# Where the rows of an expert norm are permuted: by the multiply that writes them, or by the transposes that read them

## The chip, the cores and the metric

The kernel runs on one core of one Trainium2 chip. The metric is the device time of one execution in microseconds (us). The core's engines are named as in the profile: PE is TensorE (PEld are its weight loads, which overlap with its matmuls), DVE is VectorE, ACT is ScalarE, POOL is GpSimd, SP issues most of the DMA transfers.

## The reference

A decoder trunk of two layers on x of 512 tokens by 1024 features, all float32. Each layer is a mixer (layer 0: mLSTM heads beside differential attention; layer 1: a gated convolution), then a mixture of experts, each behind an RMSNorm; a last RMSNorm ends it. What matters here is the part around the experts, cut:

```python
h = rmsnorm(x, norm_ffn[layer])            # y = x * rsqrt(mean(x*x) + eps) * g
glog = t @ wg + bg                         # t = h as 512 x 1024; 4 groups
elog = t @ we + be                         # 16 experts, 4 per group
# top-1 group, then top-2 experts within it, softmax weights
for e in range(16):
    y = (silu(t @ w_gate[e]) * (t @ w_up[e])) @ w_down[e]   # 1024 -> 512 -> 1024
    out = out + combine[:, e:e + 1] * y
x = x + out
```

## The kernel before

Tokens lie in four tiles of 128 rows (`TT = 4`), the features in eight blocks of 128 (`KD = 8`). PE contracts over partitions, so each normed tile, token by feature, has to be turned: eight 128 by 128 transposes, each of which loads one block of the tile as weights (a PEld instruction) and streams an identity through it.

There are five norms, n = 0 to 4. The even ones stand ahead of the mixers and at the end. The odd ones, n = 1 and n = 3, are the expert norms. The weights of gate, up and router are fetched with `rearrange("(p k) n -> p k n")`: partition p holds the features 8p to 8p + 7, so block k of the contraction is every eighth feature, k, k + 8, k + 16, and so on. The odd norms therefore write their rows permuted: the DVE multiply of `norm` (one scalar_tensor_tensor per tile, line 913) reads x and the gain in order and writes feature 8p + k at position 128k + p of `h_rows`, neighbouring results 512 bytes apart. Everything after it reads blocks of 128 contiguous columns:

* `turn_h(n, t)` (line 1386) turns tile t, for the routing logits (`logits`, line 1607). For the odd norms it is called in `project_out`, between the tiles of the mixer's output projection: tiles (1,0), (1,1), `turn_h` 0, tile (1,2), `turn_h` 1, `logits` 0, tile (1,3), `turn_h` 2, `logits` 1, `turn_h` 3, `logits` 2 and 3.
* POOL stores the four tiles to `h_dram` (line 514). After routing it gathers, for each expert, up to 96 of those rows (`CAP = 96`) by an indirect DMA into `xg` (line 521), two buffers in turn.
* `turn_xg(n, u)` (line 1650) turns the 96 gathered rows of one expert, eight transposes of 96 by 128. ACT copies the result out of PSUM rounded to fp32r (line 743), DVE subtracts to get the remainder (line 1237).

A projection is three fp32r matmuls (`mm3`, lines 1404 to 1406): high by high, low by high, high by low. The weights come in as float32 by SP into a ring, ACT rounds each chunk (line 569) and DVE takes the remainder (line 875).

One step of the expert loop on PE, written out by hand in `step`: the gate matmuls of expert e, `turn_act` of e - 1, the up matmuls of e, `turn_xg` of e + 1, the down matmuls of e - 1. There are 16 experts per layer and two layers, so 32 calls of `turn_xg`, 256 transposes; `turn_h` of the odd norms has 8 calls, 64 transposes.

A branch for experts with more than 96 tokens (line 1731) has the same transposes.

Of the kernel before, what the change touches and what calls it, by code (L numbers as in the profile page):

```python
# [31 lines left out]
P = 128  # L32
# [3 lines left out]
KD = D // P  # L36
# [8 lines left out]
CAP = 96  # L45
# [27 lines left out]
def hybrid_trunk(nc, A, out):  # L73
    ctx = ExitStack()
    with ctx:
# [12 lines left out]
        ident = sb("ident", [P, P])  # L88
# [60 lines left out]
        h_rows = part(0, TT, D)  # L149
# [14 lines left out]
        xg = part(8192, 2, D)  # L164
# [224 lines left out]
        def turn_bank(n, t):  # L389
            return 2 * (t % (2 if n else 3))  # L390
# [465 lines left out]
        def _(dve):  # L856
# [27 lines left out]
            def norm(n, finish_x=None, ahead=0, copies=True):  # L884


                def copy(t):
                    b, cs = turn_bank(n, t), slice(t * P, (t + 1) * P)
                    if n % 2 == 0:
                        dve.wait_ge(tr_act, n * TT + t + 1)  # L890
                        ins = v.tensor_tensor(hT[:, 1, :, cs], ps[:, b:b + 2, :].rearrange("p b (k c) -> p (b k) c", k=4),
                                              hT[:, 0, :, cs].bitcast(F32), ALU.subtract)
                    else:
                        dve.wait_ge(tr_full, 2 * (n * TT + t) + 2)
                        ins = v.tensor_copy(hT_route[:, 4:8, cs], ps[:, b + 1, :].rearrange("p (k c) -> p k c", k=4))
                    ins.then_inc(tr_dve, 1)

                if finish_x and ahead:
                    finish_x(0)
                for t in range(TT):  # L900
                    if finish_x and t + ahead < TT:
                        finish_x(t + ahead)
                    if t == 0 and n == 0:
                        dve.wait_ge(first_gain_loaded, 16)
                    elif t == 0:
                        dve.wait_ge(gain_loaded, 16 * n)
                    dve.wait_ge(norm_rstd, n * TT + t + 1)
                    row, h_row, gains = x_sb[:, t, :], h_rows[:, t, :], gain[:, :]
                    if n % 2:

                        row, gains = (a.rearrange("q (p k) -> q p k", k=KD) for a in (row, gains))
                        h_row = h_row.rearrange("q (k p) -> q p k", k=KD)
                    ins = v.scalar_tensor_tensor(out=h_row, in0=row, scalar=st[:, 4 + t:5 + t],  # L913
                                                 in1=gains, op0=ALU.mult, op1=ALU.mult)
                    ins.then_inc(h_ready, 1)
                    if copies and t and n:
                        copy(t - 1)
                if n == 0:

                    copy(0)  # L920
                    splits(2)
                    copy(1)
                    splits(PIECE)
                    copy(2)
                    splits(at_start(0))
                    copy(3)
                elif copies:
                    copy(TT - 1)
# [444 lines left out]
        def _(pe):  # L1373
            mm = nc.tensor.matmul

            def turn_h(n, t):

                pe.wait_ge(h_ready, n * TT + t + 1)
                reuse = 2 if n else 3
                if t >= reuse:  # L1380
                    pe.wait_ge(tr_act, n * TT + t + 1 - reuse)
                    pe.wait_ge(tr_dve, n * TT + t + 1 - reuse)
                for b in range(2):
                    for k in range(4):
                        c = 4 * b + k
                        last = nc.tensor.transpose(ps[:, turn_bank(n, t) + b, k * P:(k + 1) * P],  # L1386
                                                   h_rows[:, t, c * P:(c + 1) * P], ident[:, :])
                    last.then_inc(tr_full, 1)

            def norm(n):  # L1390
# [235 lines left out]
            def route(l):  # L1626
# [10 lines left out]
                for e in range(E):  # L1637
# [5 lines left out]
                    if e % 4 == 3:  # L1643
                        last.then_inc(idx_full, 1)

            def turn_xg(n, u, landed_value):

                pe.wait_ge(xg_landed[u], landed_value)
                for k in range(KD):
                    last = nc.tensor.transpose(ps[:, 5 + k // 4, (k % 4) * P:(k % 4) * P + CAP],  # L1650
                                               xg[0:CAP, u, k * P:(k + 1) * P], ident[0:CAP, 0:CAP])
                last.then_inc(xg_turned, 1)

            def gate_or_up(bank, u, c, i):
# [33 lines left out]
            def experts(l):  # L1688
                n0, c0 = E * l, step_chunk(l, 0)
                turn_xg(n0, 0, 16 * (n0 // 2 + 1))  # L1690
                gate(n0, 0, c0, None)
                turn_xg(n0 + 1, 1, 16 * (n0 // 2 + 1))
                gate_or_up(1, 0, c0 + 4, None)

                def step(n, u, c, i, landed_next, first=False, last=False):

                    gate(n, u, c, i)
                    turn_act(n - 1)
                    gate_or_up(1, u, c + 4, i)
                    if not last:  # L1700
                        turn_xg(n + 1, 1 - u, landed_next)
                    down(n - 1, 1 - u, c + 8, i, first)

                for e in (1, 2):
                    n = n0 + e
                    step(n, e % 2, step_chunk(l, e), None, 16 * ((n + 1) // 2 + 1), first=(l == 0 and e == 1))
                with pe.Fori(0, E // 2 - 2) as i:
                    for u in range(2):
                        step(i * 2 + (3 + u + n0), 1 - u, step_chunk(l, 3) + 12 * u, i,
                             i * 16 + 16 * ((4 + u + n0) // 2 + 1))  # L1710
                n = n0 + E - 1
                step(n, 1, step_chunk(l, E - 1), None, None, last=True)
                turn_act(n)
                down(n, 1, step_chunk(l, E), None)

                o = over[l]
                pe.wait_ge(flag_ready, l + 1)
                with pe.If(pe.value_load(overflow_flag[0:1, l:l + 1], min_val=0, max_val=1) > 0):
                    pe.wait_ge(y_act, n0 + E)
                    pe.wait_ge(y_dve, n0 + E)  # L1720
                    with pe.Fori(0, E * OVER) as it:
                        w8 = w_over.rearrange("p (k n) -> p k n", k=KD)
                        w4 = w_over.rearrange("p (k n) -> p k n", k=KF)
                        pe.wait_ge(o["sel"], it + 1)
                        for t in range(TT):
                            last = mm(ps[0:CAP, 0, 0:1], sel_over[:, t, 0:CAP], tok_id[:, t:t + 1],
                                      start=(t == 0), stop=(t == TT - 1))
                        last.then_inc(o["idx_full"], 1)
                        pe.wait_ge(o["xg"], it * 16 + 16)
                        for k in range(KD):  # L1730
                            last = nc.tensor.transpose(ps[:, 1 + k // 4, (k % 4) * P:(k % 4) * P + CAP],
                                                       xg[0:CAP, 0, k * P:(k + 1) * P], ident[0:CAP, 0:CAP])
                        last.then_inc(o["turned"], 1)
                        pe.wait_ge(o["xgT"], it + 1)
                        for m in range(2):
                            pe.wait_ge(o["w"], it * 48 + 16 * (m + 1))
                            for k in range(KD):
                                last = mm(ps[0:CAP, 3 + m, :], xgT_over[:, k, 0:CAP], w8[:, k, :],
                                          start=(k == 0), stop=(k == KD - 1))
                            last.then_inc(o["done"], 1)  # L1740
                        pe.wait_ge(o["act"], it + 1)
                        for k in range(KF):
                            last = nc.tensor.transpose(ps[:, 5, k * P:k * P + CAP], act_h[0:CAP, k * P:(k + 1) * P],
                                                       ident[0:CAP, 0:CAP])
                        last.then_inc(o["act_turned"], 1)
                        pe.wait_ge(o["actT"], it + 1)
                        pe.wait_ge(o["w"], it * 48 + 48)
                        for half in range(2):
                            for k in range(KF):
                                last = mm(ps[0:CAP, 6 + half, :], actT_over[:, k, 0:CAP], w4[:, k, half * 512:half * 512 + 512],  # L1750
                                          start=(k == 0), stop=(k == KF - 1))
                        last.then_inc(o["done"], 1)
# [39 lines left out]
```

## Time and profile before

| | |
|---|---|
| median of 3 runs | 1253.16 us (1252.01 to 1254.99) |
| the profiled execution | 1254.11 us, its span 1252.4 us |
| PE busy | 1088.5 us, 87% of the span |
| DVE busy | 864.5 us, 69% |
| ACT busy | 655.3 us, 52% |
| granted PE clock, mean over the span | 0.917 |
| HBM | 267.57 MB read, 20.20 MB written |

The span is the part of the execution that the profiler records, 1.7 us less than the execution's time. Busy shares are means over stages that differ: the two expert loops, from about 375 to 660 us and from about 923 to 1210 us, are nearly half of the span. The granted clock is given as a share of 2.4 GHz: 1.00 is 2.4 GHz and 0.50 is 1.2 GHz. Durations of PE instructions contain a latency that overlaps with the next instruction, so the pace, start to start, says what a row of them costs.

### The profile page before, as it was taken

To read this page: it belongs to the slowest core of one execution; us is meant where nothing else is said; L and a number is where in the kernel's file an instruction comes from. 1 tells how busy PE (TensorE), PEld (TensorE's weight loads), DVE (VectorE), ACT (ScalarE), POOL (GpSimd) and SP (SyncE) were. 2 spreads that over 40 slices of the span, in tenths; PEclk is the share of its full clock that TensorE was granted. 3 is DMA by queue.
4 is the path that set the end of the run, shared out by engine and by line. 5 is a ranking of instruction groups with operands and counts; after the bars stand their busy time and mean duration, and the time that the engine had idled before them with its cause. 6 is when DMAs were issued, how large, how long until landed. Compare 5 with 4: busy or idle time off the path is not lost.

```text
span 1252.4 us, 14773 instructions
## 1 busy us (share of the span) xinstructions
PE 1088.5 (87%) x5104; PEld 819.8 (65%) x5104; DVE 864.5 (69%) x1067; ACT 655.3 (52%) x809; POOL 115.3 (9%) x159
## 2 busy tenths in 40 slices
PE   5999994896958999999993699999849999999980
PEld 4776772675855777777772587878746777777750
DVE  5254545365566999999994544354559999999964
ACT  5233434352315888888882322223317888888851
POOL 2000000120020100000002100000111000000005
PEclk8999997698958999999997699999859999999995
DMA  8632212003235999999993723223318999999945
GB/s 293 187 114 76 76 68 68 18 1 134 74 135 178 374 398 410 399 398 398 409 406 121 293 68 116 86 75 127 129 44 302 399 407 399 397 398 407 411 172 207
DMA packets 78828, 287.10 MB, mean 229 GB/s; under 512 B 16663, under 2 KB 16663, under 8 KB 62396
## 3 DMA queue, kind: packets, MB, share of 16 engines
q1 hardware_dynamic: 66236, 241.64, 50.8%
q0 software_dynamic: 8816, 31.73, 7.6%
q10 hardware_dynamic: 3728, 13.11, 2.7%
q8 instruction: 28, 0.46, 0.1%
q14 instruction: 20, 0.16, 0.0%
HBM read 267.57 MB, written 20.20 MB: 230 GB/s over the span
## 4 chain that ended last, share of the span: by engine, by line
PE 81%; DVE 8%; ACT 4%; DMA 3%; issue 2%; POOL 1%; ACTq 0%; POOLq 0%; SPq 0%; PEldq 0%; DVEq 0%
PE ps L1404 24%; PE ps L1406 24%; PE ps L1405 24%; PE ps L1650 2%; PE ps L1607 1%; DVE x_sb L1149 1%; DMA arena<-h_rows_dram,arena 1%; DVE w_split L875 1%; DVE arena L913 1%; PE ps L1495 1%; PE ps L1541 1%; ACT w_split L569 1%; DMA arena<-y_rows_dram,arena 1%; PE ps L1516 1%; PE ps L1672 1%
## 5 line engine op out<-in xcount | busy, mean ns | idle before, releaser
L875 DVE TENSOR_TENSOR w_split<-ring,w_split 128x1024 fp32r<-128x1024 f32 x452 | 540.1, 1220 | 105.6 <-ACT w_split L569 93.7
L569 ACT CAST w_split<-ring 128x1024 fp32r<-128x1024 f32 x452 | 472.9, 1052 | 223.5 <-PE ps L1406 221.5
L1404 PE MATMUL ps<-w_split,hT 128*96 128x512 f32 (+1 forms) x960 | 385.7, 402 | 17.5 <-DVE hT L1244 6.2
L1405 PE MATMUL ps<-w_split,hT 128*96 128x512 f32 (+1 forms) x960 | 379.7, 396 | 0.0
L1406 PE MATMUL ps<-w_split,hT 128*96 128x512 f32 (+1 forms) x960 | 379.6, 395 | 0.0
L1404 PEld LDWEIGHTS ps<-w_split,hT 128*96 128x96 f32 (+1 forms) x960 | 162.5, 169 | 79.1 <-DVE hT L1244 6.6
L1406 PEld LDWEIGHTS ps<-w_split,hT 128*96 128x96 f32 (+1 forms) x960 | 162.2, 169 | 61.9
L1405 PEld LDWEIGHTS ps<-w_split,hT 128*96 128x96 f32 (+1 forms) x960 | 162.7, 169 | 56.5
L1404 PE MATMUL ps<-hT,w_split 128*128 128x512 f32 x352 | 141.1, 401 | 4.4 <-issue 2.4
L1405 PE MATMUL ps<-hT,w_split 128*128 128x512 f32 x352 | 138.7, 394 | 0.0
L1406 PE MATMUL ps<-hT,w_split 128*128 128x512 f32 x352 | 138.6, 394 | 0.0
L521 POOL DMA_INDIRECT arena<-h_rows_dram,arena x32 | 42.0, 1313 | 468.8 <-PE ps L1650 424.8
L1404 PEld LDWEIGHTS ps<-hT,w_split 128*128 128x128 f32 x352 | 67.1, 191 | 26.5 <-issue 11.0
L1406 PEld LDWEIGHTS ps<-hT,w_split 128*128 128x128 f32 x352 | 67.0, 190 | 14.5
L1405 PEld LDWEIGHTS ps<-hT,w_split 128*128 128x128 f32 x352 | 67.3, 191 | 13.5
L619 ACT ACTIVATE arena<-x_sb 128x1024 f32<-128x1024 f32 x20 | 21.2, 1058 | 72.4 <-DVE x_sb L1149 34.3
L1386 PE MATMUL ps<-ident,arena 128*128 128x128 f32 x128 | 24.0, 350 | 38.9 <-DVE arena L913 38.2
L913 DVE SCALAR_TENSOR_TENSOR arena<-x_sb,st,arena 128x1024 f32<-128x1024 f32 x20 | 31.8, 1592 | 29.9 <-POOL st L463 29.9
L1386 PEld LDWEIGHTS ps<-ident,arena 128*128 128x128 f32 x128 | 19.8, 182 | 42.9 <-DVE arena L913 31.1
L460 POOL TENSOR_SCALAR st<-st 128x1 f32<-128x1 f32 (+1 forms) x28 | 11.5, 410 | 389.6 <-ACT arena L619 252.3
L743 ACT CAST hT<-ps 128x768 fp32r<-128x768 f32 x32 | 25.4, 793 | 32.3 <-PE ps L1650 32.3
L666 ACT ACTIVATE x_sb<-x_sb,st 128x128 f32<-128x128 f32 (+3 forms) x32 | 17.7, 555 | 46.2 <-DVE st L1009 46.2
(197 smaller groups left out, 814.4 us busy)
## 6 DMA issues: line engine op xcount, KB each, us to landing
ring<-in_exp_w_gate SPq DMA_DIRECT2D x64, 1024.0 KB, 11.0
ring<-in_exp_w_up SPq DMA_DIRECT2D x64, 1024.0 KB, 10.7
ring<-in_exp_w_down SPq DMA_DIRECT2D x64, 1024.0 KB, 11.6
ring<-in_w_in_even SPq DMA_DIRECT2D x14, 1024.0 KB, 9.4
y_rows_dram<-arena ACTq DMA_DIRECT2D x32, 384.0 KB, 7.0
ring<-in_w_in_odd SPq DMA_DIRECT2D x12, 1024.0 KB, 8.7
ring<-in_w_out_even SPq DMA_DIRECT2D x4, 1024.0 KB, 5.0
h_rows_dram<-arena POOLq DMA_DIRECT2D x8, 512.0 KB, 4.4
```

The costliest lines, as they stand in the source:

```text
L521: g.indirect_dma_start(out=xg[0:CAP, e % 2, :], out_offset=None, in_=h_dram, in_offset=bass.IndirectOffsetOnAxis(ap=slot_tok[0:CAP, e:e + ...
L569: s.copy(hi_of(c), raw(c)).then_inc(hi_ready, 1)
L619: s.activation(junk, x_sb[:, t, :], ACT.Square, accum_out=st[:, t:t + 1]).then_inc(sumsq_ready, 1)
L666: s.activation(e_maps[:, u % 2, m, 0:n], e_maps[:, u % 2, m, 0:n], ACT.Exp, bias=st[:, 16 + c:17 + c], accum_out=st[:, 20 + c:21 + c]).the ...
L743: s.copy(xgT[:, u, 0, :, 0:CAP], ps[:, 5:7, :].rearrange("p b (k c) -> p (b k) c", k=4)[:, :, 0:CAP]).then_inc(xgT_act, 1)
L875: v.tensor_tensor(lo_of(c), raw(c), hi_of(c).bitcast(F32), ALU.subtract).then_inc(lo_ready, 1)
L913: ins = v.scalar_tensor_tensor(out=h_row, in0=row, scalar=st[:, 4 + t:5 + t], in1=gains, op0=ALU.mult, op1=ALU.mult)
L1386: last = nc.tensor.transpose(ps[:, turn_bank(n, t) + b, k * P:(k + 1) * P], h_rows[:, t, c * P:(c + 1) * P], ident[:, :])
L1404: mm(out, a[0], b[0], start=start, stop=False)
L1405: mm(out, a[1], b[0], start=False, stop=False)
L1406: return mm(out, a[0], b[1], start=False, stop=stop)
L1650: last = nc.tensor.transpose(ps[:, 5 + k // 4, (k % 4) * P:(k % 4) * P + CAP], xg[0:CAP, u, k * P:(k + 1) * P], ident[0:CAP, 0:CAP])
```

## The change

The multiply of `norm` writes all its rows in feature order. The transposes of the odd norms' tiles and of the gathered rows load their block as every eighth column of the row, neighbours 32 bytes apart. No instruction is added or removed and no wait moves.

```diff
                     row, h_row, gains = x_sb[:, t, :], h_rows[:, t, :], gain[:, :]
-                    if n % 2:
-
-                        row, gains = (a.rearrange("q (p k) -> q p k", k=KD) for a in (row, gains))
-                        h_row = h_row.rearrange("q (k p) -> q p k", k=KD)
                     ins = v.scalar_tensor_tensor(out=h_row, in0=row, scalar=st[:, 4 + t:5 + t],
...
                         c = 4 * b + k
-                        last = nc.tensor.transpose(ps[:, turn_bank(n, t) + b, k * P:(k + 1) * P],
-                                                   h_rows[:, t, c * P:(c + 1) * P], ident[:, :])
+                        block = (h_rows[:, t, :].rearrange("q (p k) -> q k p", k=KD)[:, c, :] if n % 2
+                                 else h_rows[:, t, c * P:(c + 1) * P])
+                        last = nc.tensor.transpose(ps[:, turn_bank(n, t) + b, k * P:(k + 1) * P], block, ident[:, :])
...
+            def xg_block(u, k):
+                return xg[0:CAP, u, :].rearrange("q (p k) -> q k p", k=KD)[:, k, :]
+
             def turn_xg(n, u, landed_value):
...
                     last = nc.tensor.transpose(ps[:, 5 + k // 4, (k % 4) * P:(k % 4) * P + CAP],
-                                               xg[0:CAP, u, k * P:(k + 1) * P], ident[0:CAP, 0:CAP])
+                                               xg_block(u, k), ident[0:CAP, 0:CAP])
```

The branch for crowded experts gets the same edit.

## Rows read from the trace of the kernel before

**Rows 1.** The page: the chain that ended last, by engine and by line.
```profile
PE 81%; DVE 8%; ACT 4%; DMA 3%; issue 2%; POOL 1%; ACTq 0%; POOLq 0%; SPq 0%; PEldq 0%; DVEq 0%
PE ps L1404 24%; PE ps L1406 24%; PE ps L1405 24%; PE ps L1650 2%; PE ps L1607 1%; DVE x_sb L1149 1%; DMA arena<-h_rows_dram,arena 1%; DVE w_split L875 1%; DVE arena L913 1%; PE ps L1495 1%; PE ps L1541 1%; ACT w_split L569 1%; DMA arena<-y_rows_dram,arena 1%; PE ps L1516 1%; PE ps L1672 1%
```
**Rows 2.** Windows over the two expert loops.
```profile
core 0: us, PE busy (x) PEld busy (x) DVE busy (x) ACT busy (x) POOL busy (x), PEclk, DMA share, GB/s
375.00:660.00 285.00, 278.56 (x1315) 198.59 (x1316) 262.21 (x265) 226.06 (x249) 17.22 (x16) 0.98 0.95 371
923.00:1210.00 287.00, 279.38 (x1332) 199.45 (x1332) 262.77 (x269) 225.23 (x248) 19.12 (x17) 0.98 0.93 361
```
**Rows 3.** Waits of PE, 377 to 659 us: total, times, longest.
```profile
PE ps L1650 <- DMA arena<-h_rows_dram,arena: 2.6, 1, 2.6
PE ps L1404 <- DVE hT L1237: 1.9, 1, 1.9
```
**Rows 4.** Line 913: an odd norm (323 to 350 us), then norm 0 (ns min/median/max).
```profile
L913 DVE SCALAR_TENSOR_TENSOR arena<-x_sb,st,arena x4: 1958/2086/2099, 325.9 to 345.8; 128x1024 f32<-128x1024 f32 x4
...
L913 DVE SCALAR_TENSOR_TENSOR arena<-x_sb,st,arena x4: 1283/1284/1286, 8.3 to 14.3; 128x1024 f32<-128x1024 f32 x4
```
**Rows 5.** Line 1352, the same operation on half the row.
```profile
L1352 DVE SCALAR_TENSOR_TENSOR arena<-arena,conv_sb x16: 750/752/754, 739.3 to 823.6; 128x512 f32<-128x512 f32 x16
```
**Rows 6.** Timeline around the end of the first odd norm: start us, us, engine.
```profile
343.20 1.06 PE L1386 MATMUL ps<-ident,arena 128*128 128x128 f32 x8 [0.30 <-PE ps L1406]
...
344.10 1.86 PE L1607 MATMUL ps<-w_route,arena 128*128 128x20 f32 x16
...
345.84 1.96 DVE L913 SCALAR_TENSOR_TENSOR arena<-x_sb,st,arena 128x1024 f32<-128x1024 f32 x1 [2.12 <-POOL st L463]
...
347.86 1.95 PE L1386 MATMUL ps<-ident,arena 128*128 128x128 f32 x8 [1.90 <-DVE arena L913]
...
349.60 6.86 PE L1607 MATMUL ps<-w_route,arena 128*128 128x20 f32 x32
```
**Rows 7.** Timeline around the first odd norm's first turn.
```profile
325.87 2.08 DVE L913 SCALAR_TENSOR_TENSOR arena<-x_sb,st,arena 128x1024 f32<-128x1024 f32 x1 [2.22 <-POOL st L463]
...
328.21 1.04 PE L1386 MATMUL ps<-ident,arena 128*128 128x128 f32 x8
```
**Rows 8.** Timeline around one turn of gathered rows in the loop.
```profile
478.80 0.87 PEld L1650 LDWEIGHTS ps<-ident,arena 96*128 96x128 f32 x8
...
479.03 0.82 PE L1650 MATMUL ps<-ident,arena 96*128 96x96 f32 x8
...
479.64 0.45 PE L1404 MATMUL ps<-w_split,hT 128*96 128x512 f32 x1
```
**Rows 9.** Line 1650 from 385 to 660 us (ns min/median/max).
```profile
L1650 PEld LDWEIGHTS ps<-ident,arena x120: 138/141/143, 388.3 to 637.7; 96*128 96x128 f32 x120
L1650 PE MATMUL ps<-ident,arena x120: 244/246/247, 388.6 to 637.8; 96*128 96x96 f32 x120
```
**Rows 10.** Weight loads of line 1404 of 128 and of 36 columns.
```profile
L1404 PEld LDWEIGHTS ps<-hT,w_split x352: 186/188/331, 43.9 to 842.6; 128*128 128x128 f32 x176
...
L1404 PEld LDWEIGHTS ps<-hT,w_gates_split x8: 109/112/112, 67.5 to 72.2; 128*36 128x36 f32 x8
```
**Rows 11.** Line 1607 from 323 to 345.9 us.
```profile
L1607 PEld LDWEIGHTS ps<-w_route,arena x32: 190/192/192, 335.3 to 345.7; 128*128 128x128 f32 x32
```
**Rows 12.** Timeline, the first turn of a layer's gathered rows.
```profile
377.40 1.25 PEld L1650 LDWEIGHTS ps<-ident,arena 96*128 96x128 f32 x8 [2.71 <-DMA arena<-h_rows_dram,arena]
377.40 1.54 PE L1650 MATMUL ps<-ident,arena 96*128 96x96 f32 x8 [2.62 <-DMA arena<-h_rows_dram,arena]
```
**Rows 13.** Windows after the third turn of the odd norm.
```profile
346.00:348.00 2.00, 0.14 (x1) 0.14 (x2) 2.00 (x2) 0.00 (x0) 1.43 (x3) 0.98 0.90 344
348.00:350.00 2.00, 2.00 (x11) 2.00 (x11) 0.47 (x2) 0.15 (x1) 0.53 (x1) 0.50 0.97 383
```
**Rows 14.** The remainder after that turn in Rows 8.
```profile
482.05 0.95 DVE L1237 TENSOR_TENSOR hT<-ps,hT 128x768 fp32r<-128x768 f32 x1
```

More of the change, by code:

```diff
@@ L1731, in experts @@
                             last = nc.tensor.transpose(ps[:, 1 + k // 4, (k % 4) * P:(k % 4) * P + CAP],
-                                                       xg[0:CAP, 0, k * P:(k + 1) * P], ident[0:CAP, 0:CAP])
+                                                       xg_block(0, k), ident[0:CAP, 0:CAP])
                         last.then_inc(o["turned"], 1)
```

## Prediction

> **What bounds the kernel now.** I read the chain that ended last first, for who sets the end; then the windows and the waits of the two stages in which the change has most of its instructions; then the touched lines one by one, with their neighbours in the timeline.
>
> The chain is PE for 81% of the span, and almost all of that are the three lines of `mm3`; the turns of gathered rows are 2% of it, some 25 us, the multiply of `norm` 1% [rows 1]. In the expert loops PE is busy 278.6 of 285 us and 279.4 of 287 us [rows 2], and in the whole of the first loop its two largest waits are one of 2.6 us and one of 1.9 us, both in its start-up [rows 3]. So PE is the bound there: a nanosecond added to it is added to the end, and one taken from DVE is not given back. DVE has 262 of the 285 us and the transfers a share of 0.95 [rows 2], but both follow PE's pace and would only wait longer for a slower PE.
>
> **The multiply.** It removes the scattered write of 8 multiplies. Strided, one takes 2086 ns; contiguous, as norm 0 has it, 1284 ns [rows 4]. That is 0.80 us each, 6.4 us of DVE time. What is it worth? Only where somebody waits. Tile 0: the multiply ends at 325.87 + 2.08 = 327.95, the turn starts its matmuls at 328.21 straight behind the projection's, with no wait [rows 7]: nothing. Tiles 1 and 2 likewise have projection tiles in front of their turns. Tile 3: PE waits 1.90 us for the multiply of 1.96 us [rows 6]. With 1.28 us it ends 0.68 us sooner, so 2 layers x 0.68 = **1.4 us gained**. The stores of the rows and the gathers have no more to do than before (rows of 4 KB either way), and between tile 3 and the first turn of gathered rows lies the whole of the routing, so an earlier store is worth nothing.
>
> **The turns, as they are.** A turn of gathered rows: its matmuls start at 479.03 and 8 of them end 0.82 us later, one taking 0.246 [rows 8, 9], so the pace is (0.82 - 0.246)/7 = 82 ns. A load in it takes 141 ns [rows 9] and lies under the matmul before it; the first even starts at 478.80, 0.23 us ahead of its matmul, under the last matmul of the projection [rows 8]. How much of a load's 141 ns is streaming? Loads of 128 and of 36 columns take 188 and 112 ns [rows 10]: 0.83 ns a column and 82 ns fixed. A load of a transpose then streams for 141 - 82 = 59 ns, 23 ns less than the pace, and the matmul sets the pace. That loads can set it is seen in `logits`, where the matmul has 20 columns: 16 take 1.86 us, with loads of 192 ns [rows 6, 11]; the pace (1.86 - 0.19)/15 = 111 ns is the load's 192 - 82 = 110 ns.
>
> In `turn_h` of the odd norms the pace at the full clock is (1.04 - 0.27)/7 = 110 ns (0.27 being one matmul, estimated as the 246 ns of 96 columns plus 2 cycles at 2.4 GHz for each of 32 more) [rows 7, 9].
>
> **What a load of every eighth column costs.** The trace has no strided read by PE. Bounds: from below nothing, 59 ns, since nothing excludes it. The nearest row is the multiply's own scattered write. Contiguous multiplies of 1024 and 512 columns take 1284 and 752 ns [rows 4, 5], so 1.04 ns a column and 220 ns fixed; the strided one then has (2086 - 220)/1024 = 1.82 ns a column. Three readings of it for 128 columns:
> (a) as a ratio (1.75) or a plain doubling of the load's stream: 103 to 118 ns;
> (b) as an addition of 0.78 ns a column: 59 + 100 = 159 ns;
> (c) as the time that one access to a place of its own takes, whoever makes it: 128 x 1.82 = 233 ns.
> I take (c). The strided write is 1.75 of its engine's own column times, which is no whole number of them, so it looks like a time set by the memory and not by the engine; and PE, at 0.46 ns a column, asks for the columns faster than DVE and would feel such a time more. It is a write of one engine taken for a read of another, so all of (a), (b) and (c) stay in the range.
>
> The Trainium skill ("Advanced Engine Details and Errata", SBUF Cachelines) says that the memory is read in lines of 16 bytes, that accesses which share a line run at full speed and need at least two hits on it, and that an access to a new line each time pays a penalty, which it does not size. Four float32 share such a line in a contiguous block and none in the new one, so by the page the change is a loss. The slower scattered write [rows 4] agrees in kind.
>
> **The sum, with (c).** Loads of consecutive transposes follow each other at 233 ns, matmuls under them.
> 1. In each layer 15 of the 16 turns of gathered rows run at the full clock: the first load starts 0.23 us early as now and costs nothing, the other seven set the pace: 7 x (233 - 82) = 1.05 us. Times 30: 31.7 us.
> 2. The first turn of each layer follows a wait for the gather, at the lower clock: its pace now is (1.54 - 0.42)/7 = 160 ns [rows 12] (0.42 being the first, cold matmul, an estimate from 0.246 and the halved clock). 7 x 73 = 0.5, and the first load lies open, some 0.1 more: 1.2 us for both.
> 3. `turn_h` 0 and 1 of each layer stand in a full row of projection matmuls: 7 x (233 - 110) = 0.86 each, 3.4 us for four.
> 4. `turn_h` 2 gets 0.86 us longer too, but is followed by `logits` 1 and then by the wait of 1.90 us [rows 6]. The multiply takes 0.68 of this cover, the turn 0.86, and 0.36 is left: nothing. If the cover were gone it would cost its excess.
> 5. `turn_h` 3 is at the lower clock [rows 6, 13], pace (1.95 - 0.42)/7 = 219 ns against 233: 0.1 plus 0.1 for the open first load, 0.4 for both layers.
> 6. The multiply: -1.4.
> Sum: 31.7 + 1.2 + 3.4 + 0.4 - 1.4 = **+35.3 us**. The profiled execution took 1254.1 us, 0.9 more than the median; against the median of 1253.2 the forecast is **1288 us**.
>
> Who waits behind the longer turn? ACT's copy and DVE's remainder, which is done at 482.05 + 0.95 = 483.0 [rows 14]. PE needs it after 24 down matmuls; behind the first at 479.64 [rows 8], at the spacing of 0.23 us by which the first load ran ahead, they end about 485.2, so it has 2.2 us of cover, and both ends shift alike. The gather of the expert after next starts later by the same 1 us and each step is longer by it.
>
> **The rivals.**
> R1, the stride is free, or hidden: PE is not made slower, the end comes 1.4 us sooner, 1252 us. This is the case that ends on the other side. The mechanism is that a load has 23 ns to grow under the matmul. It decides from 82 ns: a load of 82 ns costs nothing, one of 89 ns (210 loads x 7 ns = 1.4) makes it even. For it: nothing in the trace shows PE paying for a stride. Against it: DVE pays 75% for one [rows 4, 5]. A variant gives a real gain: PE's idle 1.90 us ahead of `turn_h` 3 shrinks, and the clock, 0.98 in that wait and 0.50 in the 2 us after it [rows 13], stays up; then the 6.86 us of `logits` 2 and 3 become 2 x 1.7 [rows 6] and the turn 1 us less, up to 4.4 us a layer, 1243 us. The same shortening of the wait happens in my forecast, where it could take up to 9 us off; but the activity before it is then turns and `logits` alone, as now, so I leave it out of the sum and in the range.
> The Trainium skill ("TensorE: Matmul & The Clock Gate", LDWEIGHTS) ties a load's time to its number of columns alone, columns by 1.2 GHz. By it 128 columns are 107 ns (an estimate from the page) contiguous or not. The loads of `mm3`, 0.83 ns a column [rows 10], agree; a transpose's 59 ns do not.
> R2, the load doubles or grows by the ratio, (a): 118 ns. 7 x 36 x 30 = 7.6, four `turn_h` 7 x 8 x 4 = 0.2, minus 1.4: +6.4, **1260 us** (with 103 ns +3.0, 1256).
> R3, the load grows by DVE's addition, (b): 159 ns. 7 x 77 x 30 = 16.2, `turn_h` 1.4, minus 1.4: +16, **1269 us**.
> R4, a strided load also stops lying under a matmul: pace 233 + 82 = 315 ns, 8 x 233 = 1.9 us a turn: 56 for 30 turns, 7.5 for four `turn_h`, some 5 for the rest, minus 1.4: +67, **1320 us**. Against it: nothing in the trace shows a load waiting for the matmul ahead.
>
> **How the numbers follow.** Forecast 0.44; R1 0.17 (of it 0.04 with the gain of the clock); R2 0.20; R3 0.12; R4 0.07. About 0.2%, 2.5 us, is what a measurement of this kernel can tell from no change. R1 without the clock is inside it (0.13), R2 at its lowest end adds 0.01; the rest is slower: 0.82. The forecast's own range is 1281 to 1295 (a place of its own at 1.67 to 1.9 ns a column, the clock a few us either way). Cases of both signs are not balanced, but to leave out no more than 2 in 10 the range must reach to R1: 1251 to 1297.
>
> **What would show it.** The multiplies of the odd norms at 1284 ns. The loads of lines 1386 (odd norms) and 1650 longer: 82 + 233 = 315 ns under (c), 200 under R2, 240 under R3, 141 under R1; a turn of gathered rows 1.9 us from first to last instead of 0.82. PE's idle ahead of `turn_h` 3 down from 1.90 to about 0.4 us. Loads and matmuls of `mm3` unchanged. The forecast is wrong if the load's record is below 170 ns, if the loops' ends do not move by the sum of the turns, or if the granted clock inside the loops falls below 0.98.

## The result and the profile after

The changed kernel takes 1258.5 us (median of 5 runs, 1258.05 to 1262.11) against 1252.41 us (5 runs). The ratio is 1.0043, 95% interval 1.0031 to 1.0055: 5.4 us slower (3.9 to 6.9). The profiled execution took 1258.05 us, its span 1256.3 us.

In the changed kernel the multiply is line 909, `turn_h` line 1384, `logits` line 1604, `mm3` lines 1401 to 1403; `turn_xg` stays line 1650. The multiply, over all norms, and the turns of gathered rows in the first loop (ns min/median/max):

```profile
L909 DVE SCALAR_TENSOR_TENSOR arena<-x_sb,st,arena x20: 1271/1283/1286, 8.2 to 1250.3; 128x1024 f32<-128x1024 f32 x20
```
```profile
L1650 PEld LDWEIGHTS ps<-ident,arena x112: 186/204/207, 406.3 to 638.2; 96*128 96x128 f32 x112
L1650 PE MATMUL ps<-ident,arena x112: 247/274/276, 406.5 to 638.3; 96*128 96x96 f32 x112
```

All 20 multiplies are as quick as the contiguous one of [rows 4]. The loads have grown from 141 to 204 ns [rows 9], far from the 315 ns forecast. The timeline around a turn:

```profile
477.34 1.09 PEld L1650 LDWEIGHTS ps<-ident,arena 96*128 96x128 f32 x8
477.58 1.02 PE L1650 MATMUL ps<-ident,arena 96*128 96x96 f32 x8
```

Eight matmuls span 1.02 us instead of 0.82 [rows 8]: a pace of (1.02 - 0.274)/7 = 107 ns instead of 82, and 0.20 us more per turn. That this goes undiminished into the pace of the loops is read from the same two turns in both kernels, 13 steps apart, in the first loop and in the second. In the kernel before:

```profile
408.74 0.82 PE L1650 MATMUL ps<-ident,arena 96*128 96x96 f32 x8
...
637.19 0.82 PE L1650 MATMUL ps<-ident,arena 96*128 96x96 f32 x8
...
958.89 0.82 PE L1650 MATMUL ps<-ident,arena 96*128 96x96 f32 x8
...
1187.34 0.82 PE L1650 MATMUL ps<-ident,arena 96*128 96x96 f32 x8
```
and in the changed one:
```profile
406.49 1.02 PE L1650 MATMUL ps<-ident,arena 96*128 96x96 f32 x8
...
637.54 1.02 PE L1650 MATMUL ps<-ident,arena 96*128 96x96 f32 x8
...
960.05 1.02 PE L1650 MATMUL ps<-ident,arena 96*128 96x96 f32 x8
...
1191.10 1.02 PE L1650 MATMUL ps<-ident,arena 96*128 96x96 f32 x8
```

The changed kernel is 2.25 us ahead at the first and 0.35 us behind at the second, 2.60 us lost over 13 steps of the loop: 0.20 a step. In the second loop it goes from 1.16 to 3.76 us behind, 2.60 us again. Over 30 warm turns that is 6.0 us. The lead itself is mostly no gain of the change: 1.54 us of it were there at the first turn of the odd norm (326.67 against 328.21 [rows 7]), ahead of which the two kernels differ only in a multiply for which nobody waits.

The end of the first odd norm, whose rows before are [rows 6]:

```profile
342.56 1.86 PE L1604 MATMUL ps<-w_route,arena 128*128 128x20 f32 x16
344.25 1.28 DVE L909 SCALAR_TENSOR_TENSOR arena<-x_sb,st,arena 128x1024 f32<-128x1024 f32 x1 [2.13 <-POOL st L463]
...
345.59 1.48 PE L1384 MATMUL ps<-ident,arena 128*128 128x128 f32 x8 [1.17 <-DVE arena L909]
```

The multiply is 0.68 us shorter, PE's wait 1.17 instead of 1.90 us. It shrinks by what the multiply gives up and by the 0.06 us by which `turn_h` 2 has grown (1.12 instead of 1.06 us). The last turn takes 1.48 instead of 1.95 us: part of it still has the full clock, as the window over it shows (columns as in [rows 2]):

```profile
345.00:347.00 2.00, 1.41 (x10) 1.41 (x10) 1.14 (x2) 0.00 (x0) 1.36 (x3) 0.81 0.83 324
347.00:349.00 2.00, 2.00 (x12) 2.00 (x10) 1.02 (x2) 1.89 (x3) 0.00 (x0) 0.50 1.02 403
```

Then the clock falls to 0.50 as before [rows 13]. In the second layer the last turn takes 1.97 us in both kernels, so the clock gave something back in one layer only.

### The profile page after: what moved, and what is told of

Same layout as the page of the kernel before. It is cut to its first block, busy times and chain, and to the rows that moved or that the text cites. A ratio compares the mean times of both kernels' runs of the same rounds, so it can differ in the third digit from the quotient of the medians.

```text
span 1256.3 us, 14773 instructions
## 1 busy us (share of the span) xinstructions
PE 1095.2 (87%) x5104; PEld 828.2 (66%) x5104; DVE 862.0 (69%) x1067; ACT 655.5 (52%) x809; POOL 114.5 (9%) x159
## 3 DMA queue, kind: packets, MB, share of 16 engines
q1 hardware_dynamic: 66236, 241.64, 50.6%
## 4 chain that ended last, share of the span: by engine, by line
PE 81%; DVE 8%; ACT 4%; DMA 3%; issue 2%; POOL 1%; ACTq 0%; POOLq 0%; SPq 0%; PEldq 0%; DVEq 0%
PE ps L1401 24%; PE ps L1403 23%; PE ps L1402 23%; PE ps L1650 2%; PE ps L1604 1%; DVE x_sb L1145 1%; DVE w_split L875 1%; DMA arena<-h_rows_dram,arena 1%; PE ps L1492 1%; DVE arena L909 1%; ACT w_split L569 1%; PE ps L1538 1%; DMA arena<-y_rows_dram,arena 1%; PE ps L1513 1%; PE ps L1672 1%
## 5 line engine op out<-in xcount | busy, mean ns | idle before, releaser
L1403 PEld LDWEIGHTS ps<-hT,w_split 128*128 128x128 f32 x352 | 67.0, 190 | 14.4
L909 DVE SCALAR_TENSOR_TENSOR arena<-x_sb,st,arena 128x1024 f32<-128x1024 f32 x20 | 25.6, 1282 | 29.8 <-POOL st L463 29.8
## 6 DMA issues: line engine op xcount, KB each, us to landing
ring<-in_exp_w_gate SPq DMA_DIRECT2D x64, 1024.0 KB, 11.6
```

Source lines behind the costliest of these rows:

```text
L1403: return mm(out, a[0], b[1], start=False, stop=stop)
```

## The experiments

Ratios are against runs of the kernel before on the same chip, and times in microseconds are worked from the ratio and 1250 us. Kernels with mispaired features route their tokens otherwise than the reference; the fixed 96 rows for each expert keep the amount of work, and in none of the traces does the branch for crowded experts run. Kernels that were made for their trace alone ran once.

**The multiply alone.** The permutation is taken out of the multiply and nothing is put in its place.

```diff
-                    if n % 2:
-                        row, gains = (a.rearrange("q (p k) -> q p k", k=KD) for a in (row, gains))
-                        h_row = h_row.rearrange("q (k p) -> q p k", k=KD)
```

> The multiply writes in order, the turns load contiguous blocks as before; the contraction then pairs features with other features' weights, so this times the gain alone. Theory (the loss comes from the turns of gathered rows alone, the gain is PE's shorter wait at the third tile of each odd norm): 1.4 us below the kernel before by the 0.68 us per layer, up to 2.5 us if the clock falls later too, as the changed kernel showed (its lead grew by 1.2 and 1.05 us across the two odd norms); turns of gathered rows at 0.82 us. Rival (the order of the rows costs something elsewhere, in the stores or gathers): no gain, or above the kernel before.

Ratio 0.9996 (0.9987 to 1.0005): between 1.6 us faster and 0.6 us slower. The gain forecast, 1.4 us, is just inside; so is none. The timing neither confirms nor excludes it. Its turns have a load of 147 ns on average over all and take 0.82 us.

**The turns alone.** The changed kernel with the scattered write put back.

```diff
                     row, h_row, gains = x_sb[:, t, :], h_rows[:, t, :], gain[:, :]
+                    if n % 2:
+                        row, gains = (a.rearrange("q (p k) -> q p k", k=KD) for a in (row, gains))
+                        h_row = h_row.rearrange("q (k p) -> q p k", k=KD)
```

> The multiply writes scattered as before, the turns load every eighth column; again features and weights are mispaired. Theory: 30 warm turns of gathered rows x 0.20 us = 6.0 us above the kernel before, turns of tiles unchanged (their matmul pace of 110 ns covers a load of 107 ns), so about 1.0048. Rival (part of the loss lies in the start-up or the tail, where the changed kernel's trace drifted by 1.3 us after the first expert loop): a different total, with the loops' sum still at 6.0.

Ratio 1.0059 (1.0046 to 1.0073): 7.4 us slower (5.8 to 9.1). The 6.0 us of the turns are inside the interval. The turns alone bring the whole of the change's loss.

**The load's own pace, for steps 1 to 8.** Seven of the eight transposes of a gathered turn take only 32 rows, which makes their matmuls short. Three kernels, each with one step for even experts and another for odd ones; that with 1 and 8 is:

```diff
+                step = (1, 8)[u]
                 for k in range(KD):
+                    first = k * P if step == 1 else k
+                    rows = 32 if k else CAP
-                    last = nc.tensor.transpose(ps[:, 5 + k // 4, (k % 4) * P:(k % 4) * P + CAP],
-                                               xg[0:CAP, u, k * P:(k + 1) * P], ident[0:CAP, 0:CAP])
+                    last = nc.tensor.transpose(ps[:, 5 + k // 4, (k % 4) * P:(k % 4) * P + rows],
+                                               xg[0:rows, u, first:first + 127 * step + 1:step], ident[0:rows, 0:rows])
```

> Seven of the eight transposes of a turn of gathered rows take only 32 rows, so the identity has 32 columns, the matmul is short and the load's own pace is laid open; even experts load neighbouring columns, odd experts every eighth. Seven eighths of the gathered rows' turn is left out, so the output differs. Theory (a column in a line of its own takes 0.83 ns, a contiguous one half of it): pace 55 to 60 ns for neighbours, 107 for every eighth. Rival (the load was never the bound, something else adds 25 ns): the same difference of 25 ns between the two at a higher or lower level.

> As the kernel with steps 1 and 8, with every second column for even experts and every fourth for odd ones. Line theory (16 bytes to a line, two hits hide it): step 2 as quick as neighbours, step 4 at 107 ns. Mode theory (any step but 1 takes the ordinary load of 0.83 ns a column): both at 107 ns.

> As the kernels with steps 1 and 8 and steps 2 and 4 (seven of eight transposes of a gathered turn on 32 rows, so the load's pace is open): every third column for even experts, every sixth for odd ones. Mode theory (any step but 1 takes a slow load, whatever the step): 107 to 115 ns for both. Rival (the step matters: powers of two collide in the memory, or lines of 16 bytes count): step 3 at another pace than 6, or either clearly below 107.

The seven loads in a row, in the timelines. Steps 1, then 8:

```profile
442.39 0.51 PEld L1653 LDWEIGHTS ps<-ident,arena 32*128 32x128 f32 x7 [0.27 <-issue]
...
460.11 0.84 PEld L1653 LDWEIGHTS ps<-ident,arena 32*128 32x128 f32 x7 [0.21 <-issue]
```
Steps 2, then 4:
```profile
440.55 0.90 PEld L1653 LDWEIGHTS ps<-ident,arena 32*128 32x128 f32 x7 [0.21 <-issue]
...
458.65 0.91 PEld L1653 LDWEIGHTS ps<-ident,arena 32*128 32x128 f32 x7 [0.20 <-issue]
```
Steps 3, then 6:
```profile
443.35 0.86 PEld L1653 LDWEIGHTS ps<-ident,arena 32*128 32x128 f32 x7 [0.22 <-issue]
...
461.42 1.01 PEld L1653 LDWEIGHTS ps<-ident,arena 32*128 32x128 f32 x7 [0.20 <-issue]
```

Less one load's median record (138, 200, 213, 212, 203 and 231 ns in that order) and over six gaps, the paces are:

| step in columns | 1 | 2 | 3 | 4 | 6 | 8 |
|---|---|---|---|---|---|---|
| step in bytes | 4 | 8 | 12 | 16 | 24 | 32 |
| ns per load of 128 columns | 62 | 115 | 110 | 116 | 130 | 107 |

The other turns of the same kernels repeat these rows within 0.01 us. A load of neighbours is at most 0.48 ns a column, near the 0.46 worked out ahead of the change; whether the load itself or something else sets the 62 ns, these kernels do not tell. Any step from 2 on about doubles it, and the size of the step hardly orders the rest. The Trainium skill ("SBUF — State Buffer", Door 1: The DMA port swizzle) lets a stride of up to 4 float32 go free, because accesses that hit the same line of 16 bytes at least twice run at full speed; "Advanced Engine Details and Errata" (SBUF Cachelines) of the Trainium skill has the same lines. The trace does not agree: step 2 puts two columns into each such line and costs 115 ns all the same. The line theory falls. As wholes these three kernels took 1257.6, 1261.6 and 1267.8 us, more than the kernel before, in spite of the shorter matmuls. Each turn has a new gap of 0.20 to 0.27 us where it goes from 96 rows to 32 (in brackets in the rows above), and a step of the loop takes 17.9 to 18.1 us instead of 17.57. Only the pace within the seven loads is read from them.

**An ordinary load with a step.** The logits load every eighth column of the normed rows, before these are turned.

```diff
-                        last = mm(ps[:, 4, t * NR:(t + 1) * NR], hT_route[:, k, t * P:(t + 1) * P], w_route[:, l, k, :],
+                        last = mm(ps[:, 4, t * NR:(t + 1) * NR], h_rows[:, t, k::KD], w_route[:, l, k, :],
```

> The logits load every eighth column of the normed rows instead of a contiguous block of the turned ones, so the logits, and with them the routing, are not those of the reference. Their loads are no transposes and set the pace (111 ns). Mode theory (a transpose's contiguous load has a quick mode that a step switches off, the ordinary load already runs at 0.83 ns a column and keeps that): pace stays 111 ns, records 192. Rival (a step doubles any load): 82 + 214 = 296 ns and a pace of 215.

One call of `logits` at the full clock. It has eight products in the code and sixteen loads and matmuls in the trace:

```profile
334.28 3.88 PEld L1607 LDWEIGHTS ps<-w_route,arena 128*128 128x128 f32 x16
334.39 3.87 PE L1607 MATMUL ps<-w_route,arena 128*128 128x20 f32 x16
```
```profile
L1607 PEld LDWEIGHTS ps<-w_route,arena x21: 312/335/336, 334.3 to 345.8; 128*128 128x128 f32 x21
```

(3.88 - 0.335)/15 = 236 ns instead of 111 [rows 6, 11]; the kernel as a whole took 1262.0 us in one execution. My theory that a transpose has a quick mode which a step switches off, and that an ordinary load has nothing to lose, falls too. A step about doubles either kind, from its own level. The price is nearer to a factor (107 over 62 is 1.7, 236 over 111 is 2.1) than to an added time (45 and 125 ns) or to one time per column (0.84 ns in a turn, 1.84 ns in the logits).

**The version that reads with the step in the multiply.** x and gain are read every eighth column and the permuted row is written contiguously, so the same values are computed.

```diff
-                        row, gains = (a.rearrange("q (p k) -> q p k", k=KD) for a in (row, gains))
-                        h_row = h_row.rearrange("q (k p) -> q p k", k=KD)
+                        row, gains = (a.rearrange("q (p k) -> q k p", k=KD) for a in (row, gains))
+                        h_row = h_row.rearrange("q (k p) -> q k p", k=KD)
```

> The odd norms' multiply walks in the order of its output: it reads x and the gain every eighth column (32 bytes apart) and writes the permuted row contiguously; everything behind it is as in the kernel before. Theory (a read of scattered places costs less than a column's 1.04 ns on this engine, only the scattered write is slow): multiplies at 1284 ns, the time of the multiply-alone kernel, 0 to 2 us below the kernel before. Rival (scattered access costs 1.82 ns a column in either direction): 2086 ns, no change; with two strided inputs counted one after the other up to 3 us a multiply, and 2 us slower in all.

Ratio 1.0002 (0.9988 to 1.0016), no difference. The multiplies of the first odd norm:

```profile
L913 DVE SCALAR_TENSOR_TENSOR arena<-x_sb,st,arena x4: 2054/2222/2374, 325.7 to 345.6; 128x1024 f32<-128x1024 f32 x4
```

2222 ns against 2086 with the scattered write [rows 4]. The theory that DVE reads scattered places for nothing falls; the rival holds. With the step on x alone:

```diff
-                        row, gains = (a.rearrange("q (p k) -> q p k", k=KD) for a in (row, gains))
-                        h_row = h_row.rearrange("q (k p) -> q p k", k=KD)
+                        row = row.rearrange("q (p k) -> q k p", k=KD)
+                        h_row, gains = (a.rearrange("q (k p) -> q k p", k=KD) for a in (h_row, gains))
```

> The odd norms' multiply reads only x every eighth column; the gain is read and the row written contiguously, so the gain meets other features and the output differs. With both inputs strided a multiply took 2.2 us. Theory (each strided operand has its own port and the slowest sets the pace): 2.0 to 2.2 us with one. Rival (the two strided reads share one path): between 1.28 and 1.75 us.

```profile
L913 DVE SCALAR_TENSOR_TENSOR arena<-x_sb,st,arena x4: 2051/2177/2261, 326.9 to 346.9; 128x1024 f32<-128x1024 f32 x4
```

One strided input costs nearly what two cost (the kernel as a whole took 1250.8 us in one execution), so the two do not add up. Whether a strided input and a strided output together cost more than one of them, no run here shows.

**No permutation at all.** The weights are fetched in blocks of 128 rows, so that rows and blocks stay in order and the same values are computed. The permutation is taken out of the multiply as in the first experiment (not shown again here).

```diff
-            gate_up = [A[name][l, bass.ds(e, 1)].rearrange("a (p k) n -> p (a k) n", p=P)
+            gate_up = [A[name][l, bass.ds(e, 1)].rearrange("a (k p) n -> p (a k) n", p=P)
...
-                    (w_route[:, l, :, 0:GROUPS], A["router_group_w"][l].rearrange("(p k) n -> p k n", p=P)),
-                    (w_route[:, l, :, GROUPS:NR], A["router_expert_w"][l].rearrange("(p k) n -> p k n", p=P)),
+                    (w_route[:, l, :, 0:GROUPS], A["router_group_w"][l].rearrange("(k p) n -> p k n", p=P)),
+                    (w_route[:, l, :, GROUPS:NR], A["router_expert_w"][l].rearrange("(k p) n -> p k n", p=P)),
```

> No permutation anywhere: gate, up and router weights are fetched in blocks of 128 consecutive rows (each partition gets eight pieces of 2 KB instead of one of 16 KB), so rows and blocks stay in order. Theory (PE sets the loops' pace and the down weights, fetched in such pieces already, land in 11.6 us against 11.0): the time of the multiply-alone kernel, 0 to 2 us below the kernel before. Rival (transfers are busy at a share of 0.95 in the loops, shorter pieces push them over): PE waits for chunks, tens of us slower.

Ratio 1.0124 (1.0104 to 1.0145), 15.5 us slower: the rival's kind of loss. The first loop now, the landing of gate weights (us, median), the chain that ended last, and ACT's longest waits from 377 to 659 us (total, times, longest):

```profile
375.00:660.00 285.00, 274.82 (x1288) 193.82 (x1289) 250.94 (x259) 214.87 (x244) 20.47 (x16) 0.98 0.98 360
```
```profile
ring<-in_exp_w_gate SPq DMA_DIRECT2D x64, 1024.0 KB, 14.6
```
```profile
PE 51%; DMA 27%; DVE 11%; ACT 5%; issue 4%; POOL 1%; SPq 0%; ACTq 0%; DVEq 0%; POOLq 0%; PEldq 0%
```
```profile
ACT w_split L569 <- DMA ring<-in_exp_w_up: 22.7, 17, 2.4
```

The same window held 278.6 us of PE work at a transfer share of 0.95 and 371 GB/s [rows 2]; now the transfers are at 0.98 and carry 360 GB/s. DMA has 27% of the chain instead of 3% [rows 1], and ACT waits for weights in the loop, which it never did in the kernel before. One transfer of 1 MB takes four rows of weights for each partition, 8 KB in one piece before and four of 2 KB now (the packets of SP's queue rise from 66236 to 115388, three more for each partition of the 128 transfers); the 16 KB that the expectation names are two transfers, and the down weights come in pieces of 4 KB. These land in 14.4 us instead of 11.6 although their fetch is unchanged, so part of the longer landing is waiting behind the others. The long pieces that the permutation pays for are worth more than the permutation costs.

**The turns dealt out.** If the loss is a load that lies open under a matmul too short for it, it must vanish under a longer one. The eight transposes of the next expert are put one by one behind each third up matmul. In the changed kernel:

```diff
-            def gate_or_up(bank, u, c, i):
+            def gate_or_up(bank, u, c, i, turned=None):
...
                     if k % 2 == 1:
                         last.then_inc(chunk_done, 1)
+                    if turned:
+                        v, landed_value = turned
+                        if k == 0:
+                            pe.wait_ge(xg_landed[v], landed_value)
+                        last = nc.tensor.transpose(ps[:, 5 + k // 4, (k % 4) * P:(k % 4) * P + CAP],
+                                                   xg_block(v, k), ident[0:CAP, 0:CAP])
+                        if k == KD - 1:
+                            last.then_inc(xg_turned, 1)
...
-                    gate_or_up(1, u, c + 4, i)
-                    if not last:
-                        turn_xg(n + 1, 1 - u, landed_next)
+                    gate_or_up(1, u, c + 4, i, None if last else (1 - u, landed_next))
```

> The changed kernel, with the eight transposes of the next expert's gathered rows dealt out one by one between the up matmuls of the expert loop (one behind every third matmul) instead of in a row behind them. Theory (the loss is only that a load of 107 ns lies open under a matmul of 82 ns; under a matmul of 0.23 us it is hidden): each transpose costs its own 82 ns again, 28 of the 30 warm turns are dealt out, so 28 x 0.20 = 5.6 us come back: 0.9985 to 1.000 of the kernel before. Rival (a strided load costs TensorE its extra time wherever it stands, or each switch between projection and transpose costs more than it hides): 1.004 or above, the loop's step not shorter than 17.77 us.

The same in the kernel before, with its contiguous block in place of `xg_block(v, k)`:

> The kernel before with the same dealing out. Theory: the loads were hidden already, so nothing changes apart from the switches: 0.999 to 1.001, a step of 17.57 us. If each of the eight switches to and fro costs what the one behind a turn costs now (0.06 us longer spacing of the first matmul after it), 28 x 7 x 0.06 = 12 us are lost, and the kernel above shares that loss. If the two kernels then differ by less than 2 us, the load's extra time is hidden in both.

Ratios 1.0007 (0.9998 to 1.0015) and 1.0009 (0.9999 to 1.002). The changed kernel's loss of 0.43% is gone, and with the turns dealt out both orders take the same time. Their loads in the first loop, changed order, then the order of before:

```profile
L1667 PEld LDWEIGHTS ps<-ident,arena x112: 189/190/195, 403.6 to 638.1; 96*128 96x128 f32 x112
L1667 PE MATMUL ps<-ident,arena x112: 246/246/248, 403.8 to 638.3; 96*128 96x96 f32 x112
```
```profile
L1667 PEld LDWEIGHTS ps<-ident,arena x112: 138/140/143, 399.3 to 633.5; 96*128 96x128 f32 x112
```

The strided loads are still 50 ns longer, but the matmul's record is back at 246 ns. One step of the loop, from `turn_act` to `turn_act` eleven steps later, is 17.57 us before, 17.77 changed, and now, in the changed order:

```profile
438.02 0.49 PE L1680 MATMUL ps<-ident,arena 96*128 96x96 f32 x4
...
631.84 0.49 PE L1680 MATMUL ps<-ident,arena 96*128 96x96 f32 x4
```

(631.84 - 438.02)/11 = 17.62 us. In the other, 433.75 to 627.27 give 17.59. Of the 0.20 us a step 0.03 is left between the two orders. The loss of 0.06 us at each switch between up matmuls and transposes, which the expectation feared, is not there: the step of the order of before grows by 0.02 us for eight.

## Why the prediction was wrong

The direction and the mechanism held, the size of one term did not: 35 us forecast, 5.4 measured, inside the wide range but far from the point.

* **PE bounds the loops, and what a turn loses the end loses:** right. 0.20 us a step, unabsorbed, and 6.0 us for 30 turns.
* **A contiguous load streams 59 ns under a matmul pace of 82:** right; laid open it measures 62 or less.
* **The price of a strided load was the step that failed.** Of three readings of DVE's scattered write I took (c), an absolute time of 1.82 ns a column, 233 ns a load. It measures 107 ns, 0.84 ns a column, which is (a). The argument for (c) was that 1.75 is no whole number of DVE's column times and so looks like a time of the memory. The logits refute it: the same step on the same rows costs 1.84 ns a column there and 0.84 in a turn, so there is no one time per access, and TensorE's own ratios, 1.7 and 2.1, are no whole numbers either. Taken for its factor, 1.75, the same row would have given 103 ns, near the 107. That is no proof of the factor: for the logits it would give 194 ns, while (c)'s 233 is near the 236 that they measure. The prediction also reads a load's record as 82 ns and its stream. The record of 204 would then be a pace of 122, and it is 107.
* **Term 1** shrinks with it from 31.7 to 6.0 us. **Term 2** is nothing: the first turns of the two layers take 1.55 and 1.54 us instead of 1.54 [rows 12], as the matmul's 160 ns at the lower clock are well above 107. **Term 3** is nothing: `turn_h` has a matmul pace of 110 ns and the load now takes 107; the first two turns of the norm take 1.05 and 1.04 us. **Term 4** is nothing as forecast, but the wait behind it kept 1.17 us and not about 0.4, since `turn_h` 2 grew by 0.06 us and not by 0.86. **Term 5** is nothing: in the second layer that turn takes 1.97 us before and after.
* **Term 6, the multiply:** its 0.68 us are in the trace, 1.4 us for both layers. The clock that falls later gave the profiled execution about 0.5 us more in the first layer, where the last turn of the odd norm ran in 1.48 us, and nothing in the second. By timing, the multiply alone gives between 1.6 us faster and 0.6 slower, so how much of it reaches the end stays open; the first gather behind it varies more from execution to execution (5.0 to 7.5 us in the chains of the profiled ones).
* **The sum with the measured terms:** 6.0 - 1.4 = 4.6 us, against 5.4 (3.9 to 6.9). R2, at its price of 103 ns, said +3.0, at 118 ns +6.4. It was the right case, given 0.20.

## What to carry to other kernels

Before a block is loaded with a step, compare the doubled load with the matmul that stands over it: 107 ns under 110 cost nothing, under 82 they cost 25 ns a transpose, and it is the turns with fewer rows (96) that paid. A load that has outgrown its matmul can be put behind a longer one; that took the loss away, though it won nothing over the kernel before. And where a price is known only from another engine, hold its factor and its absolute time as about equally likely: here the factor came out in the turns and the absolute time in the logits.

## What the hardware showed

* A step of 2 columns (8 bytes) already costs TensorE's load of float32 nearly the full price: 115 ns against 62; steps 3 to 8 lie between 107 and 130, step 6 highest, step 8 lowest. Under a longer matmul nearly all of it is hidden: with step 8 a step of the loop takes 17.62 us, with neighbours 17.59.
* An ordinary float32 load of 128 columns goes from 111 to 236 ns with a step of 8, and each product has two such loads in the trace (128 for 64). Why its level is twice that of a transpose's load no run here tells.
* On VectorE a strided operand costs about 0.8 us per 1024 columns whether it is read or written: 2086 ns scattered write, 2177 one strided input, 2222 two, 1284 none.
* With pieces of 2 KB instead of 8 KB for gate and up weights, a transfer of 1 MB of gate weights lands in 14.6 us instead of 11.0, the queues being busy at a share of 0.98.
